# Where GpSimd's weight sums run, and when the key stage's row chain starts, in a one-core decoder layer

## The reference

```python
merged = sigmoid(gate_mla) * o_mla + sigmoid(gate_lru) * o_lru
x = x + rmsnorm(merged @ w_out, g_post_mix)
h = rmsnorm(x, g_pre_x);  mn = rmsnorm(mem, g_mem)
cq, ck, cv = h @ w_cq, mn @ w_ck, mn @ w_cv       # 2048 x 512 each
...                                               # softmax attention, @ w_co
x = x + rmsnorm(co @ w_co, g_post_x)
up = causal_dwconv(rmsnorm(x, g_pre_ffn) @ w_up, w_fconv, b_fconv)   # 2048 x 11264
gate, val = split(up)
x = x + rmsnorm((gelu(gate) * val) @ w_down, g_post_ffn)             # 5632 x 2048
```

## Time and profile before

| | us |
|---|---|
| median of three runs | 1707.53 (1706.75 to 1710.29) |
| the profiled execution's own time | 1707.76 |
| its span, first to last instruction | 1705.7 |
| TensorE matmul busy | 1694.7 |
| VectorE busy | 1292.7 |
| ScalarE busy | 980.2 |
| GpSimd busy | 266.4 |

### The profile page before, as it was taken

How to read it: one execution, slowest core, us unless ns; L and a number is a source line. 1 busy time by engine, 2 the same in 40 slices (tenths; PEclk the granted TensorE clock), 3 DMA queues, 4 the chain that set the end, 5 groups by cost and what they waited for, 6 DMA issues and landing times.

```text
span 1705.7 us, 24655 instructions
## 1 busy us (share of the span) xinstructions
PE 1694.7 (99%) x8887; PEld 1453.0 (85%) x8887; DVE 1292.7 (76%) x1638; ACT 980.2 (57%) x1238; POOL 266.4 (16%) x340
## 2 busy tenths in 40 slices
PE   9999999999999999999999999999999999999998
PEld 7888888888888888888888888888888888888887
DVE  7766675468788897676887687778877778977797
ACT  6656655454577765455556575556545555545554
POOL 0012212220245431101211101110001110001100
PEclk9999999999999999999999999999999999999999
DMA  9644459997555649799999755556765556765555
GB/s 345 204 131 150 151 189 293 319 269 221 165 184 177 186 166 329 206 346 280 270 323 278 217 198 186 185 185 215 244 199 178 185 196 207 235 204 193 197 176 212
DMA packets 230873, 375.06 MB, mean 220 GB/s; under 512 B 8721, under 2 KB 165009, under 8 KB 228753
## 3 DMA queue, kind: packets, MB, share of 16 engines
q1 hardware_dynamic: 210992, 326.66, 56.9%
q0 software_dynamic: 13888, 32.51, 9.5%
q10 hardware_dynamic: 5920, 14.94, 2.3%
HBM read 369.89 MB, written 36.70 MB: 238 GB/s over the span
## 4 chain that ended last, share of the span: by engine, by line
PE 94%; DVE 2%; DMA 2%; ACT 1%; issue 1%; POOL 0%; SPq 0%; DVEq 0%; ACTq 0%; POOLq 0%
PE ps L636 48%; PE ps L711 29%; PE ps L958 7%; PE ps L650 3%; PE ps L803 2%; PE ps L941 1%; PE ps L867 1%; DMA raw<-in_w_ck 1%; ACT wsp L1628 1%; DVE wsp L2009 1%; PE ps L773 1%; DMA raw<-sums 1%; PE ps L896 0%; PE ps L872 0%; PE ps L743 0%
## 5 line engine op out<-in xcount | busy, mean ns | idle before, releaser
L2009 DVE TENSOR_TENSOR wsp<-raw,wsp 128x2048 fp32r<-128x2048 f32 (+2 forms) x304 | 673.6, 2229 | 187.6 <-ACT wsp L1405 165.6
L1405 ACT ACTIVATE wsp<-raw 128x2048 fp32r<-128x2048 f32 (+2 forms) x274 | 501.9, 1842 | 133.6 <-PE ps L711 90.1
L636 PE MATMUL ps<-asp,wsp 128*128 128x512 f32 x3032 | 529.2, 336 | 0.0
L636 PEld LDWEIGHTS ps<-asp,wsp 128*128 128x128 f32 x3032 | 463.5, 188 | 62.8 <-DVE asp L2604 0.3
L711 PE MATMUL ps<-wsp,hsp 128*128 128x512 f32 x1536 | 354.0, 390 | 0.0
L711 PEld LDWEIGHTS ps<-wsp,hsp 128*128 128x128 f32 x1536 | 287.5, 188 | 59.7
L636 PE MATMUL ps<-hsp,wsp 128*128 128x512 f32 (+1 forms) x1744 | 314.4, 339 | 0.0
L636 PEld LDWEIGHTS ps<-hsp,wsp 128*128 128x128 f32 x1744 | 268.3, 188 | 36.8
L711 PE MATMUL ps<-wsp,asp 128*128 128x512 f32 x768 | 175.1, 389 | 0.0
L1416 ACT ACTIVATE cr<-ps 128x256 f32<-128x256 f32 x185 | 69.2, 380 | 180.2 <-PE ps L636 160.2
L711 PEld LDWEIGHTS ps<-wsp,asp 128*128 128x128 f32 x768 | 144.0, 188 | 29.8
(11 more groups left out here) (336 smaller groups left out, 1532.7 us busy)
## 6 DMA issues: line engine op xcount, KB each, us to landing
raw<-in_w_up SPq DMA_DIRECT2D x88, 1024.0 KB, 5.4
raw<-in_w_in SPq DMA_DIRECT2D x56, 1024.0 KB, 5.4
raw<-in_w_in SPq DMA_DIRECT2D x32, 768.0 KB, 4.5
raw<-in_w_down SPq DMA_DIRECT2D x24, 1024.0 KB, 6.0
sums<-in_w_down POOLq DMA_DIRECT2D x76, 256.0 KB, 7.5
raw<-in_w_o_mla SPq DMA_DIRECT2D x16, 1024.0 KB, 9.9
raw<-in_w_o_lru SPq DMA_DIRECT2D x16, 1024.0 KB, 6.6
raw<-sums SPq DMA_DIRECT2D x31, 512.0 KB, 4.2
```

The lines of the kernel that those rows point to most:

```text
L636: mm = pe.matmul(ps[:, bank, 0:w], lhs(part, k), x[:, 0:w], start=(f and part == 0), stop=(l and part == 1))
L1405: act.activation(wsp[:, p0 % SLOTS, 0, 0:n], raw[:, p0 % SLOTS, 0:n], ACT.Copy).then_inc(hi_done, 1)
L2009: dve.tensor_tensor(wsp[:, slot, 1, 0:n], raw[:, slot, 0:n], wsp[:, slot, 0, 0:n].bitcast(F32), ALU.subtract).then_inc(lo_done, 1)
```

## The change

GpSimd's batches (21, 23) and (23, 26) now start only when TensorE has used the last made piece of the output product. The last two batches become one of five entries, (26, 31), cut in two: its ten copies are issued before GpSimd's first pair of rounds of the second up-projection, its ten adds after that pair, and GpSimd does not wait for the adds. In the key stage ScalarE's last four squares stand ahead of the high part of the third key piece, and VectorE's gains, root and first four adds ahead of its low part.

```diff
-SUM_BATCHES = [(0, 3), (3, 6), (6, 8), (8, 11), (11, 13), (13, 15), (15, 18), (18, 21), (21, 23), (23, 26), (26, 29), (29, 31)]
+SUM_BATCHES = [(0, 3), (3, 6), (6, 8), (8, 11), (11, 13), (13, 15), (15, 18), (18, 21), (21, 23), (23, 26), (26, 31)]
@@ ScalarE, key stage
             for c in range(4):
+                if c == 0:
+                    wo_square(range(4, 8))
                 hi(PH_CK, 0, c + LEAD)
                 if c == 0:
-                    wo_square(range(4, 8))
                     root2(4, 0, slice(0, 2))
                     act.wait_ge(wo_gain, 8)
                     act.dma_start(g_res, a["g_post_x"].to_broadcast([P, D])).then_inc(g_x_in, 16)
@@ VectorE, key stage
             for c in range(4):
-                lo(PH_CK, 0, c + LEAD)
                 if c == 0:
                     wo_gains(range(4, 8))
                     tok_rms(4, 0, slice(0, 2), wo_sq, 8)
                     dve.wait_ge(x2_in, 16)
                     x2_add(0)
                     x2_add(1)
+                lo(PH_CK, 0, c + LEAD)
@@ GpSimd
-            def weight_sums(first, last):
+            def weight_sums(first, last, part=None):
...
-                for at in range(first, last):
-                    for e in range(2):
-                        pool.dma_start(sums[at][:, e * 512:e * 512 + 512], block(at, 0, 0)).then_inc(sums_step, 16)
+                if part != "added":
+                    for at in range(first, last):
+                        for e in range(2):
+                            pool.dma_start(sums[at][:, e * 512:e * 512 + 512], block(at, 0, 0)).then_inc(sums_step, 16)
+                if part == "copied":
+                    return
                 step()
                 for at in range(first, last):
                     pool.dma_start(sums[at][:, 0:512], block(at, 0, 1), accum_op=ALU.add).then_inc(sums_step, 16)
                     pool.dma_start(sums[at][:, 512:1024], block(at, 1, 0), accum_op=ALU.add).then_inc(sums_step, 16)
-                step()
+                if part != "added":
+                    step()
...
             pool.wait_ge(gemm_step, PH_GL[1].g_end)
-            for batch in SUM_BATCHES[6:]:
+            for batch in SUM_BATCHES[6:8]:
+                weight_sums(*batch)
+            pool.wait_ge(gemm_step, PH_WO.g(0, PH_WO.used[WO_MADE[-1]]))
+            for batch in SUM_BATCHES[8:10]:
                 weight_sums(*batch)
@@ GpSimd, up-projection of group n
+                if n == 1:
+                    weight_sums(*SUM_BATCHES[10], part="copied")
                 up_pair(0)
+                if n == 1:
+                    weight_sums(*SUM_BATCHES[10], part="added")
                 with pool.Fori(1, up.trips // 2) as r:
                     up_pair(r)
```

## The result

The changed kernel takes 1720.41 us (median of five runs, 1718.46 to 1721.45) where the kernel before takes 1707.97 (five runs, 1706.75 to 1711.75): ratio 1.0067 [1.0056, 1.0077], **some 12 us slower**. Its profiled execution took 1718.46 us with a span of 1716.4, so 10.7 us of span are there to be found in the trace.

What follows compares the result with a forecast made beforehand. TensorE, busy in 99% of the span, was taken as the bound, with 11.0 us idle. The terms −1.35 + 1.5 + 7.5 + 1.8 = +9.45 us on 1707.76 gave 1717.2, as a median 1717.0 us; range 1706.0 to 1723.5.

Steps and rivals of the forecast that it cites:

- Part 1: Output product: moving batches (21, 23) and (23, 26) behind the last made piece costs 0, since TensorE waited for no load there.
- Part 2: Key stage: reordering lets TensorE take the third key piece at 886.5 us, not 887.86; 1.35 us won, bounds 0 and 2.05.
- Part 3: First down product: the ten copies delay the load of a plain piece; 1.5 us lost, bounds 0 and 3.
- Part 4: Second up-projection: ten adds halt GpSimd after one and eight, third product 8.5 us late; TensorE loses 7.5 us (5.3 to 13).
- Part 5: TensorE's clock after the second up-projection's gap: slow matmuls cost 1.8 us, bounds 0 and 5.5.
- the cover: Second up-projection: 1.0 us between VectorE's low part ending (1318.77) and TensorE taking that piece (1319.8).
- A: Second up-projection: the ten adds take under 22 us and fit GpSimd's gap; 1706.2 to 1707.7 us, chance 0.27.
- B: Second up-projection: the middle group of adds takes 26 us or more, product 14 late; 1724 to 1728 us, chance 0.15.
- C: Key stage: steadier loads win more than the gap there, some 4 us; 1704 us, chance 0.03.

Runs made afterwards that it cites:

- key_only: The kernel before with only the key stage's two reorderings: 1706.3 us, ratio 0.9989.
- sums_early_old_order: The kernel before with only its last four batches moved, between the output product's last made piece and the first up-projection; key stage order unchanged: 1704.71 us, repeat 1704.79.
- store_1024: The changed kernel with `dynamic_dma_scratch_size` 1024 instead of 2048: 1721.98 us, ratio 1.0086.
- copies_paced: The changed kernel with the ten copies issued two at a time, each pair after the pair before has landed: 1713.62 us, ratio 1.0029.
- copies_early: The changed kernel with the ten copies issued right after batch (23, 26), the ten adds left in place: 1712.38 us, ratio 1.0026.
- adds_eight: The changed kernel with entry 26 as an early batch of its own, leaving eight copies and eight adds in the later places: 1707.77 us, ratio 0.9993.
- adds_spread: The changed kernel with the ten adds split 4, 2 and 4 ahead of the second, third and fourth pair of rounds: 1712.98 us, ratio 1.0032.

## Why the prediction came out right, and where it did not

The sign, the size (forecast +9.45, measured +10.7 in the profile and +12.4 by the medians) and the deciding mechanism held; two terms were off by much and nearly cancelled: −1.1 in the key stage, +6.5 in the first down product, −3.9 and −0.2 in the second up-projection make up the 1.3 us between 9.45 and 10.7. That the sum came so near is luck: the first down product cost five times its forecast, and the second up-projection half of its own.

**Part 1** held: no TensorE wait came or went in the output product, and moving the sums cost 0. What it missed is that their leaving helps the stage behind, so clearing the late loads away was worth something after all.

**Part 2** had the right sign with the wrong cause. Forecast 1.35 us; measured 2.06 inside the stage (15.08 less 13.02), which is the upper bound, and 0.13 from its earlier start. The step that failed is "loads of the key, query and value weights share the DMA engines with sums as before": before, the third piece's high part waited 5.85 us for its load, and after, for nothing; the loads beside it took 12.1 us and then 6.1. key_only (one part without the other: no gain in its trace) and sums_early_old_order (the other without the one: all of it) show that the transfers' leaving did it. The prediction took that high part's start as given and did not ask what it waited for.

**Part 3** is the mis-sized term: 1.5 us forecast with bounds of 0 and 3, 8.0 measured. The upper bound took the 10.2 us of a w_out load (its own sum gives 2.6 us, called 3); the load took 13.4. Those 3.2 us more, on the bound of 3, stand near the wait of 5.65. The same ten copies in that stage cost 8.0 us with eight outstanding at once, 6.1 with seven (store_1024) and 4.0 in pairs (copies_paced), and copies_early, with none there, loses 0: as far as one execution each can show it, the cost grows with how many are outstanding. The load of the piece itself took 5.0 us beside none, 5.9 beside two, 8.7 beside four (adds_eight) and 13.4 beside eight. What part of the cost goes with the number of copies alone was not tested apart; adds_eight changed both. No row of before showed a load beside eight, so the upper end was not one. The second miss is that a half-clock stretch was charged for part 4 alone; this gap has one of 2.33 us too.

**Part 4** held in its mechanism and to the place of each halt; store_1024 (35 halts) and adds_eight (15, in other places than after the change) confirm the count where its numbers are changed. Its sizes were too high: 4.6, 19.5 and 1.1 us against 7.1, 21 and 1.4, so 4.0 us late and not 8.5. The step that failed is the first term: a single add took 2.5 us less than the row taken for it, 4.6 us in each of the change, its repeat, copies_early and adds_spread. The DMA engines' mean share was 0.37 beside it (1297 to 1301.5 us) and 0.68 beside the add of the row (693.8 to 700.9). The seven adds ran at a share of 0.97. Of the 4.0 us late TensorE lost 3.6: the cover was 0.4 us and not 1.0, since the late product itself ran 0.5 us longer (2.04 against 1.53 us).

**Part 5** held: 1.8 us forecast, 1.6 measured here, 2.3 at the other gap, and 2.8 in copies_early. The 1.8 us were an estimate from the slow matmuls at the kernel's start, where the granted clock is 1.00 (2 to 5 us): those were not slow by a lower clock, so the term came near the measured size by likeness alone. Before the change the clock is at 0.50 in the tail alone, after TensorE had been busy for 1.16 of the 4 us from 1698 on; after it, it is at 0.50 behind both waits too (1184 to 1188 and 1329 to 1331 us).

**Rivals.** A fell: the adds fill 25.1 us, over the 22 that it allowed. B fell too: its 14 us of lateness were not reached, though its 3 us for part 3 were passed by 5. C's mechanism is there, but the moves into the first down product and the second up-projection cover it: without them the kernel takes 1704.36 to 1705.18 us.

## What to carry to other kernels

Before a batch of GpSimd's transfers is put between two pieces of its work, read from the trace after how many transfers it halts, and count on from there. Here, with transfers of 256 KB and a scratch size of 2048, two counts of 14 placed every halt, one of transfers and one of units (a copy 1, an add 2), each starting anew where the next does not fit; at 1024 both were 7. Each halt lasted until all that was outstanding had landed (the next issue 0.20 to 0.40 us later). Where no halt falls, a batch takes little: the two adds at 1340.76 in adds_spread were issued within 1.7 us, the eight copies at 1163.36 in the changed kernel within 4.2. A price for a transfer's neighbours is read from a row with as many of them outstanding (the load of 1 MB took 5.0 us beside none and 13.4 beside eight), and if there is none, the upper bound is open. Where an engine waits on a load, ask first what shares the DMA engines with it (two loads of `w_ck` took 12.1 us beside GpSimd's transfers and 6.1 without), before reordering the work behind it.

## What the runs showed of the hardware that was not expected

- A load of 1 MB that takes 5.0 us takes 13.4 beside eight copies of 256 KB. While it runs, the DMA engines' mean share is 0.76 before (1169.1 to 1174.1 us) and 0.96 after (1166.3 to 1179.7 us), at 224 and 246 GB/s for all transfers together. The load's own rate, 1 MB over its time, is 210 GB/s before and 78 after.
- With the scratch size at 2048 there are 15 halts, at 1024 there are 35, with 123.3 and 259.7 us of GpSimd's time, but the kernels' times are close (1721.98 against 1720.41): TensorE's waits of 1 us and more for a low part sum to 9.3 us in the first (5.65 and 3.61) and to 11.4 in the second (7.4, 2.7 and 1.3).
- One add held GpSimd 4.6 us, six 14.4 (1291.68 to 1306.04 in adds_eight) and seven 19.5: 2.4 and 2.8 us each in a group, more alone.
- Each of TensorE's gaps of 3.6 us and more in the second group cost more than itself, and the surplus does not follow its length: 2.33 us behind 5.65, 1.59 behind 3.61, 2.8 behind 4.0 (copies_early) and 2.3 behind 7.4 (store_1024: 187.21 less 177.51 less 7.4). The gap of 2.11 us in copies_paced was followed by a granted clock of 0.50 too (1202 to 1204 us); those of 1.25 us and less in adds_eight were not.
- At a granted clock of 1.00 and with no wait, matmuls of one shape took 173 ns each in one execution of a kernel and 177 in another (sums_early_old_order and its repeat), 3 us over the first up-projection; what sets this stays open.
